# Latent attention: the values of a half in two pieces of three key tiles, one item later

## What is computed

```python
def _attend_blocks(q, k, v):                       # q: 512 tokens, k and v: 768, 16 heads
    scale = QK_HEAD_DIM ** -0.5                    # 96 numbers a head
    def one(qblk):                                 # 128 queries
        s = jnp.einsum('bqhd,bkhd->bhqk', qblk, k, preferred_element_type=jnp.float32) * scale
        p = jax.nn.softmax(s, axis=-1).astype(v.dtype)
        return jnp.einsum('bhqk,bkhv->bqhv', p, v) # 64 numbers a head
    ...
yx = _attend_blocks(q_x, k_all, v_all) @ mla_w_o[j]
```

## Time and profile before

| | us |
|---|---|
| median of 3 runs | 3264.24 |
| lowest and highest | 3261.81, 3265.47 |
| the profiled execution | 3265.15 |
| its span, first to last instruction | 3263.3 |
| mean granted TensorE clock | 0.992 |
| the items of the latent attention (from 1002.5 to 1262 us of the span) | 259.5 |
| PE busy in these | 245.5 |

### The profile page before, as it was taken

How to read it: one execution, slowest core, us unless ns; L and a number is a source line. 1 busy time by engine, 2 the same in 40 slices (tenths; PEclk the granted TensorE clock), 3 DMA queues, 4 the chain that set the end, 5 groups by cost and what they waited for, 6 DMA issues and landing times.

```text
span 3263.3 us, 40240 instructions
## 1 busy us (share of the span) xinstructions
PE 3193.4 (98%) x16204; PEld 2558.9 (78%) x16204; DVE 1624.1 (50%) x2703; ACT 1301.2 (40%) x2307; POOL 1332.4 (41%) x754
## 2 busy tenths in 40 slices
PE   7999999999998999999999999999999999999998
PEld 4876888888875557888886888888887788878886
DVE  5877376322337773432324686253432668445252
ACT  4323431222345665432334445343333544444243
POOL 2222423232253445444452234644455234464445
PEclk9999999999999999999999999999999999999999
DMA  7323334112132001423232120423333111222321
GB/s 272 105 94 126 116 110 145 56 61 67 54 120 89 14 14 47 148 81 116 72 125 84 46 62 19 147 92 96 100 88 116 52 65 49 58 95 78 116 80 56
DMA packets 85926, 288.17 MB, mean 88 GB/s; under 512 B 9803, under 2 KB 10379, under 8 KB 84972
## 3 DMA queue, kind: packets, MB, share of 16 engines
q1 hardware_dynamic: 85740, 285.60, 26.6%
HBM read 283.47 MB, written 2.10 MB: 88 GB/s over the span
## 4 chain that ended last, share of the span: by engine, by line
PE 89%; DVE 5%; issue 1%; ACT 1%; POOL 1%; DMA 1%; SPq 0%; POOLq 0%; DVEq 0%; ACTq 0%
PE ps L504 20%; PE ps L507 20%; PE ps L505 20%; PE ps L563 2%; PE ps L565 2%; PE ps L564 2%; PE ps L2131 2%; PE ps L2980 1%; PE ps L2201 1%; PE ps L1371 1%; PE ps L2571 1%; PE ps L483 1%; PE ps L478 1%; PE ps L522 1%; PE ps L479 1%
## 5 line engine op out<-in xcount | busy, mean ns | idle before, releaser
L452 POOL TENSOR_TENSOR WL<-ring,WH 128x1024 fp32r<-128x1024 f32 (+2 forms) x427 | 926.7, 2173 | 1398.4 <-ACT WH L441 1398.0
L504 PE MATMUL ps<-HX,WH 128*128 128x512 f32 x1656 | 649.7, 392 | 0.0
L507 PE MATMUL ps<-HX,WL 128*128 128x512 f32 x1656 | 648.4, 392 | 0.0
L505 PE MATMUL ps<-HX,WH 128*128 128x512 f32 x1656 | 646.8, 391 | 0.0
L441 ACT CAST WH<-ring 128x1024 fp32r<-128x1024 f32 (+2 forms) x443 | 421.2, 951 | 529.5 <-PE ps L507 471.2
L504 PE MATMUL ps<-FR,WH 128*128 128x512 f32 x1120 | 419.2, 374 | 0.3
L505 PE MATMUL ps<-FR,WH 128*128 128x512 f32 x1120 | 410.0, 373 | 0.0
L507 PE MATMUL ps<-FR,WL 128*128 128x512 f32 x1120 | 389.7, 374 | 0.0
L504 PEld LDWEIGHTS ps<-HX,WH 128*128 128x128 f32 x1656 | 311.3, 188 | 67.5 <-issue 0.8
L507 PEld LDWEIGHTS ps<-HX,WL 128*128 128x128 f32 x1656 | 312.4, 189 | 44.8
L505 PEld LDWEIGHTS ps<-HX,WH 128*128 128x128 f32 x1656 | 311.4, 188 | 44.7
(11 more groups left out here) (400 smaller groups left out, 5331.9 us busy)
## 6 DMA issues: line engine op xcount, KB each, us to landing
ring<-in_ffn_w_up SPq DMA_DIRECT2D x88, 512.0 KB, 3.4
ring<-in_w_up SPq DMA_DIRECT2D x88, 512.0 KB, 3.3
ring<-in_w_mod SPq DMA_DIRECT2D x64, 512.0 KB, 4.1
ring<-in_w_in_tok SPq DMA_DIRECT2D x40, 512.0 KB, 3.5
ring<-in_w_mod_columns SPq DMA_DIRECT2D x32, 512.0 KB, 4.4
ring<-in_w_in_feat SPq DMA_DIRECT2D x32, 512.0 KB, 3.3
ring<-in_ffn_w_down SPq DMA_DIRECT2D x32, 384.0 KB, 3.1
ring<-in_w_out SPq DMA_DIRECT2D x32, 384.0 KB, 3.1
```

The lines of the kernel that those rows point to most:

```text
L452: pool.tensor_tensor(WL[:, p % SPLITS, 0:n], ring.ap(r), WH[:, p % SPLITS, 0:n], ALU.subtract).then_inc(*ring.frees(r, split.g, "low", p))
L504: pe.matmul(o, high, xh, first, False)
L505: pe.matmul(o, high, xl, False, False)
L507: m = pe.matmul(PS[bs[i]][:, 0:N], low, get(k)[0], False, last)
```

## The change

A half's values are computed in two pieces of three key tiles in place of three pieces of two. Every piece of values, and ACT's copy of lv with it, stands one item later: part 0 (key tiles 0 to 2) in item 4v+8, nothing in item 4v+9, part 2 (key tiles 3 to 5) in item 4v+10, nothing in item 4v+11, where ACT copies lv after an odd half. The loop has one item more, 72. Work, buffers and semaphores stay as they are.

```diff
@@ lat_values_pe
-            for j in range(2 * part, 2 * part + 2):
+            for j in range(3 * part // 2, 3 * part // 2 + 3):
@@ latent
-            for i in range(71):
+            for i in range(72):
@@
-                if i >= 7:
-                    values(*divmod(i - 7, 4))
+                if i >= 8:
+                    values(*divmod(i - 8, 4))
@@ latent_pe, values
-                if v < 16 and part < 3:
+                if v < 16 and part % 2 == 0:
                     lat_values_pe(pe, v, part)
```

## The result

Six runs of the changed kernel have a median of 3274.59 us (3272.85 to 3277.68), six runs of the kernel before beside them 3264.34 (3259.00 to 3265.57). The medians are 10.25 us apart; the ratio on record, which is not that of the medians, is 1.0036, 95% interval 1.0023 to 1.0049: **slower by 0.36%, some 10 us**, against a forecast of 3263.6, outside its range and slower than every rival. The profiled execution of after took 3274.15, its span is 3272.4.

A forecast was written before the change was run, and what follows sets the result against it. PE was taken as the bound in most items, DVE in the middle of a set. Terms -0.5 - 3.4 + 0.3 + 2.0 + 1.0 = -0.6 us against the profiled 3265.15, put on the median's footing: 3263.6, range 3258.8 to 3268.6.

The forecast's parts named there:

- The end of DVE's stretch: Around items 43 to 51 and their likes: last scores come earlier, -1.15 us in each set, -3.4 in all; bounds 0, -4.2.
- Inside DVE's stretch: Items 19 to 27, 35 to 43: DVE's queue and lv's copy +0.3 us, one clock fall in item 23 or 39 +2.0.
- The last set: Items 51 to 62, PE alone the bound: three halves in fewer, longer pieces, -0.5 us; items without a piece cost nothing.
- The end: End of the stage: half 14 waits for DVE's work on lv for half 13, +1.0 us; bounds 0 and +2.
- The VT wait: Items 21 and 37: ACT's kv eviction waits about 2 us for PE to finish reading the VT buffer; costed at nothing.
- rival 3: Items 21 and 37: ACT's wait for VT reaches DVE, up to 2 us twice, 3267.6 us; chance 0.07.
- A piece of three: A values piece of three key tiles takes PE 1.45 us, against 1.02 for a piece of two.
- Rival 2: Half clock in both items 23 and 39 for 6.7 us, DVE late twice, +4.4, 3268.6 us; chance 0.16.
- signs of being wrong: ACT waits in last-set items without a piece, DVE's stretch changed by over 2 us, or half clock where none was counted.

The follow-up runs named there:

- e5: Changed kernel with DVE copying all odd heads' turns and first scores of items 11, 12, 27, 28, 43, 44 computed twice; 3267.13 us, 1.0003 to before.
- e3: Changed kernel with all copies of the odd heads' turns on DVE, in place of DVE and ACT in turn; 3272.64 us, 1.0028 to before.
- e6: Kernel before with the first scores of items 11, 27 and 43 computed three times; 3260.52 us, 0.9984 to before.
- e4: Changed kernel with the first scores of items 11, 12, 27, 28, 43 and 44 computed twice; 3271.03 us, 1.0018 to before.
- e8: e5 with the first scores of items 8, 24 and 40 computed twice as well; 3264.23 us, 0.9997 to before.
- e1: Kernel before with two pieces of three key tiles, without the shift by one item; 3262.24 us, 0.9995 to before.
- e2: Kernel before with its three pieces of two key tiles each one item later; 3276.71 us, 1.0034 to before.
- e7: e1 with the first scores of items 11, 27 and 43 computed three times; 3267.32 us, 1.0004 to before.

## Why the prediction was wrong

**"The end of DVE's stretch", -3.4: the step that failed.** Its mechanism is in the trace: the last scores of item 44 come 1.61 us earlier against item 43 (forecast 1.65), 0.14 behind the exponential. Its size holds in e5 (-3.36), where repeated scores keep the clock up and DVE makes the copies. What it lacked are the two costs that follow:

- *The half clock, 5.4 us.* The step said that the gain would be smaller by 1.7 or gone if PE came out of its wait at 1.2 GHz here too, and left that out of the sum. It came in all three sets, behind the shortened first wait and the second one that item 43 has without a piece; and the bound of 0 was too tight: with the banks' cost away and the half clock there, e3's three stretches are still 2.0 longer than before. In before the fall lay in items 11, 27 and 43 and cost 1.62 each (e6); in after it reaches items 12, 28 and 44, which have a piece of three and heads and no DVE to wait for, and costs 1.83, 1.64 and 1.96 (e4). So nothing was saved: before loses 4.8 us to its half clock, after 5.4.
- *The banks, 4.6 us.* From item 45 to 51 the step counted pieces alone (three of three against four of two). That an item without a piece costs nothing was read from item 50, in the last set, where there are no heads; there it held (windows of after, 43.46 of 44 us). In the items 13 and 15 of a set the piece was the cover for ACT's two copies of the turned heads, and lv's copy moved in ahead of them. The prediction named ACT's chain as the risk of an item without a piece, but followed the copy of lv only into item 39 and not into 15, 31 and 47.

The forecast gain was before's half clock, and nothing else: -4.8 for its removal (e6) and +1.45 for the order at an equal clock (e8 beside e6) give -3.4. An estimate of the +1.45 from the earlier trace rows: from item 12 to 18 there are four pieces of three (5.80 us) where there were five of two (5.10), since the first piece of before, in item 11, lay beside DVE; that would be 0.70 a set, more than the 0.45 to 0.55 measured.

**The first set** was left out: +1.37. In before the clock fell behind the idle time of 1.62 in item 6; in after the same 1.61 led to no fall, the next, 2.38 in item 7, did, and item 8 takes 5.33 us in place of 3.38. No run has the shift without this fall, so how much of the 1.37 is the fall is not shown. In all six kernels with the shift the fall came there, in three of the four without it behind item 6, and in e6 not at all. Why 1.6 us of idle time are enough in one and not in the other is open.

**What held.** Inside DVE's stretch: +2.27 where +0.3 + 2.0 was forecast, with one fall in the two sets, in item 40; but its parts are +0.33 in each set (0.15 forecast) and 1.6 for the fall (2.0), two misses that cancel: the sum is luck. Nor is it shown that the 0.33 is the copy of lv: e1, which leaves that copy where it was, has +0.35 in the same two stretches. The idle time before the last scores of items 24 and 40 was 1.52, not near 1.8. That the fall comes in one of the two was right in after, e3, e4 and e5, in different sets; in e2 it came in both and in e8 in none. The Trainium skill, "TensorE: Matmul & The Clock Gate", section "A second HAM failure mode: psum-queue depth-cycling", has short idles from cycling through banks as a cause of such swings. The runs agree in part: idle times of 1.45 and 1.57 us, each a wait for the single bank of the last scores, led to a fall, and e4's 0.59 and 1.18 did not, but 2.04 in e2 did not either, twice. By that rule the fall behind the stretch had to be counted too. **The last set**: -0.41 for -0.5. **The end**: +1.00, as forecast, by this chain in after (DVE's work on lv, the first piece of half 14, the output product):

```profile
1260.78 0.69 DVE L2227 TENSOR_TENSOR FR<-ps,FR 128x512 fp32r<-128x512 f32 x1 [1.69 <-ACT FR L2214]
...
1261.53 0.43 PE L2201 MATMUL ps<-T,CX 128*64 128x256 f32 x1 [1.37 <-DVE FR L2227]
...
1270.21 0.50 PE L478 MATMUL ps<-FR,WH 128*128 128x512 f32 x1
```

PE waits 1.37 for it, a wait that before did not have. **The VT wait** (rival 3) was free, as argued: ACT waits and so does PE, as timelines of after show,

```profile
1166.29 0.47 ACT L2004 ACTIVATE AR<-ps,sm 128x256 f32<-128x256 f32 x1 [1.60 <-PE ps L2201]
```

```profile
1167.18 1.98 PE L1954 MATMUL ps<-ring,AR 128*128 128x512 f32 x4 [0.94 <-ACT CX L2006]
```

but the last scores of item 24 lie +3.53 against before and those of item 19 +3.52. **A piece of three** takes 1158.91 - 1157.46 = 1.45 us, as forecast:

```profile
1157.46 0.43 PE L2201 MATMUL ps<-T,CX 128*64 128x256 f32 x1
...
1158.91 1.12 PE L2131 MATMUL ps<-AR 96*128 96x512 f32 x2
```

Rival 2 named the kind of loss, the half clock, in the wrong place: 3268.6 was worked out for the falls inside DVE's stretch. The range gave the fall behind the stretch too little room and the banks none. One of the signs of being wrong that the prediction named came true: half clock where it counted none, in items 8, 12, 28 and 44.

## What to carry to other kernels

A piece of work that is moved takes its cover along: for every item that loses one, look at what the other engines had to finish beside it in that very item, not in a similar one of a quieter stretch, and at whatever moves in with the change. Idle time taken from one wait and given to the next is not won: PE came out of two waits of 1.5 us as slow as out of one of 2.5, and then it hurt where PE was the bound. Before an order is changed to be rid of half clock, price the half clock by itself: repeating a matmul in the idle time gave 4.8 us here and told that the order had no gain to offer.

## What the runs showed of the hardware

Work that nobody needs can make the kernel faster: the first scores computed twice more, three times in the stage, kept the granted clock at 1.00 behind DVE's stretch in all three sets and made the kernel 0.16% faster (e6).

Not all half clock costs time. The stage of before has 23.9 us of it, and e6, which has none, is 4.83 us shorter. The fall in item 7 of before cost nothing: where it is absent, in e6, PE waits 1.36 us for ACT's exponential at the end of that item, and items 0 to 11 take the same time.

The idle time alone doesn't tell whether the clock falls. Behind 1.62 us in item 6 it fell in before, behind 1.61 in after it didn't; behind 2.05 in item 11 of e2 it fell, behind 2.04 in its items 27 and 43 it didn't; behind 0.73 and 1.07 in items 11 and 12 of e7 it fell in the first and third set and not in the second, and in e1, where the same two idle times come in the third set, it didn't. The runs of before differ in this too: of the 31 beside e5 to e8, the seven with a mean clock of 0.990 took 3268.1 us in the mean, the two with 0.994 took 3261.9. A fall read in one profile is a sample: a term that depends on one needs both outcomes in the range.
